# A hybrid decoder layer on one core: two pairs of output tiles by seven block products

## The chip, the cores and the metric

The kernel runs on one core of a Trainium2 chip. The metric is the device time of one execution in microseconds, taken over several runs as their median. The profile is of one execution of its own.

## The reference

One layer of a decoder, in float32, for 544 tokens (512 of a new sequence and 8 x 4 sample tokens) of 1024 channels:

```python
h = rmsnorm(x, g_pre_mix)
proj = jnp.einsum('btd,de->bte', h, w_in) + b_in        # conv, q, k, v, o, gates
y_conv = jnp.einsum('btc,cd->btd', silu(layernorm(depthwise_conv(glu(proj)))), w_conv_out)
y_m = jnp.einsum('btm,md->btd', mlstm_heads(proj), w_m_out)          # 2048 -> 1024
mix = jax.nn.sigmoid(gate_conv) * y_conv + jax.nn.sigmoid(gate_m) * y_m
x = x + rmsnorm(jnp.einsum('btd,de->bte', mix, w_o), g_post_mix)     # the output projection
hf = rmsnorm(x, g_pre_ff)
ff = jnp.einsum('btf,fd->btd', jnp.square(jax.nn.relu(hf @ w_ff1 + b_ff1)), w_ff2) + b_ff2
x = x + rmsnorm(ff, g_post_ff)
```

It also returns the new states of the convolution and of the mLSTM heads, which the change doesn't touch.

## The kernel before

**Layout.** Channels lie on the 128 partitions, tokens along the free dimension, so activations are 8 tiles (`KT`) of 128 x 544. A weight matrix is streamed as chunks of 128 output channels: `[128, 8, 128]`, 512 KB. A product of one chunk with 8 input tiles makes one output tile. For accuracy each operand is split into a high part rounded to fp32r and a low part, the rest; a product is three matmuls (high x high, high x low, low x high), and since the 544 tokens are cut in two halves of 272, a plain tile takes 8 x 3 x 2 = 48 matmuls of 272 columns.

**The ring of weights.** Every chunk has a number, its use. SyncE loads it into one of two raw buffers `wraw[0]`, `wraw[1]`; ScalarE rounds it into `whi[use % 4]` (function `hi`, L845), which is free when TensorE is through with use - 4 (`chunk_done`); VectorE subtracts to get `wlo` (`lo`, L1450) and with that frees the raw buffer (`lo_done`). TensorE waits for `lo_done` (`ring`). Both helper engines run three uses ahead of TensorE. Each engine's instructions are one queue in the order of the program text, and a wait holds all that is behind it; the order is written out by hand.

**Stages** in order of time: gated linear units, four mLSTM heads, gates, convolution output, memory output (`w_m_out`, C_MEM), output projection (`w_o`, C_OUT), MLP (C_FF).

**Seven products.** In the memory stage and in the MLP's second half some pairs of output tiles are made from 7 block products instead of 8: with the weights of two tiles and half of the inputs as a 2 x 2 block matrix, and the tokens' two halves as columns, Strassen's scheme in Winograd's form. `mem_seventh` (TensorE) makes P1, P7, P6, P5, P2, P4, P3 in this order from weight blocks X1 (P1, P7), X2 (P6, P5), X3 (P2, P4), X4 (P3), each product 4 x 3 matmuls of 272 columns. It needs sums of weight blocks (`mem_sum`, L1913 to L1922) and four sums of token blocks, which three VectorE steps make, then rounded by ScalarE and subtracted by VectorE. The banks of P1 and P7 are copied away by ScalarE before P2 and P4 add to them, and VectorE makes the part common to three results (`mem_common`) before P3. The memory pairs change between the banks `psum` (even) and `side` (odd).

**The output projection before.** `alternate` makes tiles 0 to 5 plain, each 48 matmuls, in `psum[0]` and `psum[1]` by turns. ScalarE squares (L853) and copies (L1183) each tile, VectorE adds up the squares (L2044). Tiles 6 and 7 are made by token halves: first the front half of both, then the back halves, so that the root of the front half's sum of squares (a matmul with ones, at step 3 of 8 of tile 6's back half; L1199, L1201) is ready early. Then VectorE, for each half, normalizes (L2061), adds the input (L2066) and makes low parts (L2072), which the MLP's first tiles wait for. The input comes back in one 2.1 MB load into `sgm` once all 8 mixed tiles are done. The mixed tiles `yc` (operands `bhi`, `blo`) are made in the memory stage: VectorE mixes a tile (`mix_even` L1989 to L1995, `mix_odd` L2001 to L2006), ScalarE rounds it (L1147), VectorE subtracts (L2011).

**The MLP's start.** 10 plain tiles; VectorE scales each pair's tiles by the root into `cq` (L2117, `plain_scaled`), ScalarE applies ReLU and square, and both make the 7 forms of it (`forms_made` L2125 to L2135; ScalarE L1279 to L1285). Then 27 units follow, the first with its weight splits `first_low` L2161, `sums_low` L2166, `second_low` L2173.

**The tail.** The last unit's results are squared, summed by matmuls with ones, the root is taken (L1410, L1412), then VectorE scales (L2289) quarter by quarter, the input is added (GpSimd L835 for the front half, VectorE L2301 for the back half), and each quarter is stored.

```python
def mem_bank(p, n):
    pairs = (psum[0], psum[1]) if p % 2 == 0 else (side[:, 0:2, :], side[:, 2:4, :])
...
for j in range(KT - 2):
    alternate(0, j, C_OUT, S_OUT, bhi, blo, (opnd_lo, 2 * KT) if j == 0 else None)
```

Of the kernel before, what the change touches and what calls it, by code (L numbers as in the profile page):

```python
# [12 lines left out]
P = 128  # L13
D_MODEL = 1024
KT = D_MODEL // P
SEQ = 512
# [30 lines left out]
C_FF = C_OUT + KT  # L47
# [43 lines left out]
_reads, _used, _splits = {"act": 2 * MEM_PAIRS, "dve": 2 * MEM_PAIRS}, {}, 0  # L91
# [14 lines left out]
def up_chunk(j):  # L106
    return C_FF - LATE + 2 * HID * (j // HID) + j % HID


def down_chunk(g, j):  # L110
    return C_FF - LATE + 2 * HID * (g // 2) + HID + 2 * j + g % 2


def mem_use(p, x):
    return C_MEM + len(MEM_USES) * p + MEM_USES.index(x)
# [96 lines left out]
def hybrid_layer(nc, xT, wstream, w_gates, cols, b_gates, b_v, w_dw, hist, c_in, n_in, m_in,  # L212
# [8 lines left out]
    with ctx:  # L221
# [158 lines left out]
        mem_s4 = at("mem_s4", [P, KT // 2, P], f32, late)  # L380
        mem_e = at("mem_e", [P, HALF], f32, late + TT * 4)
# [129 lines left out]
        def mem_raw_due(p, n):  # L511
            return 16 * (C_MEM // 2 + 2 * p + n + 1)

        def mem_bank(p, n):

            pairs = (psum[0], psum[1]) if p % 2 == 0 else (side[:, 0:2, :], side[:, 2:4, :])
            return pairs[n // 2][:, n % 2, 0:HALF]

# [4 lines left out]
        def mem_form(f, kt):  # L523

            if f < 3:
# [60 lines left out]
        def _(sp):  # L586
# [16 lines left out]
            def load(first, last, ahead=0):  # L603

                with sp.Fori(first, last) as i:
                    for s in range(2):
                        sp.wait_ge(lo_done, 2 * i + (s - 1 + ahead))
# [18 lines left out]
            load((C_OUT - LATE) // 2, (C_OUT - LATE + 4) // 2, LATE)  # L626

            sp.wait_ge(mixed, KT)
            sp.dma_start(sgm[:, :, :], xT).then_inc(x2_in, 16)
            load((C_OUT - LATE + 4) // 2, (C_FF - LATE) // 2, LATE)  # L630
# [11 lines left out]
            def unit_load(t):  # L642
# [7 lines left out]
                else:  # L650
                    sp.wait_ge(split_lo, SPLIT_AT[t - 2, "first"])
                    if is_down(t - 2):
                        sp.wait_ge(sum_made, MEM_SUMS * MEM_PAIRS + SUMS * order_of(t - 2) + SUMS - 1)
# [11 lines left out]
                if t >= 2:  # L665
                    sp.wait_ge(split_lo, SPLIT_AT[t - 2, "second"])
                    if is_down(t - 2):
                        sp.wait_ge(sum_made, MEM_SUMS * MEM_PAIRS + SUMS * order_of(t - 2) + SUMS)
# [15 lines left out]
            for g in range(2):  # L684
                part = slice(HALF * g, HALF * (g + 1))
                for half in range(2):
                    tiles = slice(KT // 2 * half, KT // 2 * (half + 1))
                    sp.wait_ge(out_pool if g == 0 else out_added, half + 1)
# [10 lines left out]
        def _(pool):  # L699
# [132 lines left out]
            for half in range(2):  # L832
                tiles = slice(KT // 2 * half, KT // 2 * (half + 1))
                pool.wait_ge(y_scaled, half + 1)
                pool.tensor_tensor(yacc[:, tiles, 0:HALF], yacc[:, tiles, 0:HALF], x1b[:, tiles, 0:HALF], ALU.add).then_inc(out_pool, 1)  # L835


        @block.scalar
        def _(act):
            def hi(i, per, k):  # L840

                act.wait_ge(raw_in[k % 2], 8 * per * i + 16 * ((k if k < C_OUT else k - LATE) // 2 + 1))
# [272 lines left out]
            def mem_rounded(p, x):  # L1115
# [12 lines left out]
                elif x == "X4":  # L1128
                    act.wait_ge(sum_made, MEM_SUMS * p + 4)
                    act.activation(whi[:, slot_, 0:KT // 2, :], mem_s4[:, :, :], ACT.Copy).then_inc(hi_done, 1)  # L1130
# [5 lines left out]
            def next_rounded(use):  # L1136

                if use < C_MEM or use >= C_OUT:
# [1699 lines left out]
```

## Time and profile before

| | us |
|---|---|
| median of 3 runs (1216.23 to 1217.03) | 1216.5 |
| the profiled execution | 1217.08 |
| its span, first to last instruction | 1215.6 |

| engine | busy us | share of the span |
|---|---|---|
| TensorE, matmuls | 1193.1 | 98% |
| TensorE, weight loads | 1121.5 | 92% |
| VectorE | 880.7 | 72% |
| ScalarE | 558.2 | 46% |
| GpSimd | 98.2 | 8% |

The page's chain of what ended last goes through TensorE for 93%, VectorE 3%, ScalarE 2%. The mean granted clock is 0.997 of full speed. The output projection lies between 780.4 and 829.2 us of the span.

How to read it: busy time says how full an engine is, not whether it holds the end. A wait in the profile is put down to the instruction that released it. The time of one instruction is from its start to its last write; two that don't depend on each other overlap by a little less than 0.1 us.

### The profile page before, as it was taken

The page shows a single profiled execution, that of the slowest core. Times are in us where ns is not written, and L with a number is a line of the kernel's source. Part 1 is how long each engine was busy: PE and PEld are TensorE (multiplying, and loading weights), DVE is VectorE, ACT ScalarE, POOL GpSimd, SP SyncE. Part 2 cuts the span into 40 slices and gives each one's busy share as a digit, 9 for nine tenths or more (in the row PEclk, how much of TensorE's full clock was granted, in tenths as well). Part 3 has the DMA queues.
Part 4 walks back from the last instruction along what each step waited for, and adds up shares of the span by engine and source line. Part 5 has one row for each costly group of instructions (what it writes and reads, how often), then busy time and mean ns, then how long its engine had stood idle before and what let it go on. Part 6 is the DMA issues. An engine that isn't in the chain of part 4 may idle for free.

```text
span 1215.6 us, 22805 instructions
## 1 busy us (share of the span) xinstructions
PE 1193.1 (98%) x8845; PEld 1121.5 (92%) x8845; DVE 880.7 (72%) x1329; ACT 558.2 (46%) x864; POOL 98.2 (8%) x163
## 2 busy tenths in 40 slices
PE   9999999999999999999999999999999999999995
PEld 9999978988797888879999999999999999999995
DVE  6933788988888888888458567538676577575796
ACT  7533443443355335335545333346655444354543
POOL 4120001101200110110000000000010010001111
PEclk9999999999999999999999999999999999999998
DMA  6344216516441751542322223431645445444662
GB/s 223 105 146 163 70 55 241 201 35 202 159 167 37 250 186 55 179 164 80 98 87 88 68 88 105 146 120 44 212 127 142 114 133 138 121 117 129 161 190 73
DMA packets 52623, 158.62 MB, mean 130 GB/s; under 512 B 5525, under 2 KB 7957, under 8 KB 52169
## 3 DMA queue, kind: packets, MB, share of 16 engines
q1 hardware_dynamic: 36376, 107.93, 27.2%
q0 software_dynamic: 16032, 49.62, 14.1%
q8 instruction: 50, 0.82, 0.3%
q14 instruction: 21, 0.16, 0.0%
q10 hardware_dynamic: 144, 0.09, 0.0%
HBM read 133.12 MB, written 24.49 MB: 130 GB/s over the span
## 4 chain that ended last, share of the span: by engine, by line
PE 93%; DVE 3%; ACT 2%; issue 1%; DMA 1%; DVEq 0%; ACTq 0%; SPq 0%
PE product L2307 68%; PE side L2307 24%; DMA wraw<-in_wstream 1%; ACT whi L845 0%; PE side L2492 0%; ACT yacc L1422 0%; DVE accp L1663 0%; ACT hhi L1285 0%; ACT cq L1265 0%; DVE wlo L1450 0%; DVE yacc L2192 0%; DVE hlo L2135 0%; DVE wlo L2167 0%; DVE cq L2117 0%; DVE wlo L2166 0%
## 5 line engine op out<-in xcount | busy, mean ns | idle before, releaser
L2307 PE MATMUL product<-ahi,whi 128*128 128x272 f32 x1232 | 261.7, 292 | 2.8 <-DVE cq L2117 1.6
L2307 PE MATMUL product<-ahi,wlo 128*128 128x272 f32 x1232 | 256.9, 288 | 0.0
L2307 PE MATMUL product<-alo,whi 128*128 128x272 f32 x1232 | 256.9, 288 | 0.0
L2307 PEld LDWEIGHTS product<-ahi,whi 128*128 128x128 f32 x1232 | 194.8, 188 | 13.2 <-issue 12.3
L1450 DVE TENSOR_TENSOR wlo<-wraw,whi 128x1024 fp32r<-128x1024 f32 x106 | 129.1, 1223 | 94.9 <-ACT whi L845 83.1
L2307 PEld LDWEIGHTS product<-alo,whi 128*128 128x128 f32 x1232 | 194.7, 189 | 0.0
L2307 PEld LDWEIGHTS product<-ahi,wlo 128*128 128x128 f32 x1232 | 193.5, 189 | 0.0
L845 ACT ACTIVATE whi<-wraw 128x1024 fp32r<-128x1024 f32 x106 | 111.1, 1054 | 159.5 <-PE product L2307 76.4
L1663 DVE SCALAR_TENSOR_TENSOR accp<-u,wdw,accp 128x512 f32<-128x512 f32 x240 | 163.6, 743 | 0.7 <-DVE accp L1663 0.7
L2307 PE MATMUL side<-hhi,whi 128*128 128x272 f32 x252 | 72.9, 289 | 1.8 <-DVE wlo L2161 1.3
L2307 PE MATMUL side<-hlo,whi 128*128 128x272 f32 x252 | 72.4, 287 | 0.0
L2307 PE MATMUL side<-hhi,wlo 128*128 128x272 f32 x252 | 72.4, 287 | 0.0
L828 POOL DMA_DIRECT2D wraw<-in_wstream x16 | 13.8, 863 | 595.9 <-DMA wraw<-in_wstream 595.9
L1309 ACT ACTIVATE whi<-wraw 128x1024 fp32r<-128x1024 f32 x27 | 28.6, 1059 | 69.7 <-PE side L2307 34.9
L2307 PE MATMUL product<-hhi,whi 128*128 128x272 f32 x196 | 56.6, 289 | 0.6 <-DVE hlo L2135 0.4
L2307 PE MATMUL product<-whi,ahi 128*128 128x512 f32 (+1 forms) x160 | 56.6, 354 | 0.0
L2307 PE MATMUL product<-hlo,whi 128*128 128x272 f32 x196 | 56.4, 288 | 0.0
L2307 PE MATMUL product<-hhi,wlo 128*128 128x272 f32 x196 | 56.3, 287 | 0.0
L2307 PE MATMUL product<-wlo,ahi 128*128 128x512 f32 (+1 forms) x160 | 55.8, 349 | 0.0
L2307 PE MATMUL product<-whi,alo 128*128 128x512 f32 (+1 forms) x160 | 55.8, 348 | 0.0
L2307 PE MATMUL product<-blo,whi 128*128 128x272 f32 x256 | 55.5, 288 | 0.0
L2307 PE MATMUL product<-bhi,whi 128*128 128x272 f32 x256 | 55.5, 288 | 0.0
(418 smaller groups left out, 2630.4 us busy)
## 6 DMA issues: line engine op xcount, KB each, us to landing
wraw<-in_wstream SPq DMA_DIRECT2D x176, 512.0 KB, 3.7
crg<-in_c_in POOLq DMA_DIRECT2D x32, 512.0 KB, 6.8
out_c_s<-crg POOLq DMA_DIRECT2D x32, 512.0 KB, 3.2
wraw<-in_wstream POOLq DMA_DIRECT2D x16, 256.0 KB, 4.1
s<-in_wstream SPq DMA_DIRECT2D x15, 256.0 KB, 3.9
s<-in_wstream POOLq DMA_DIRECT2D x15, 256.0 KB, 6.2
hb<-head_rows POOLq DMA_DIRECT2D x4, 580.0 KB, 5.3
x<-in_xT SPq DMA_DIRECT2D x4, 544.0 KB, 6.5
```

The lines of the kernel that those rows point to most:

```text
L828: pool.dma_start(raw_of(t)[:, 0, KT // 2:KT, :], wstream[one, :, 0:KT // 2, :], accum_op=ALU.add).then_inc(s3_in[d % 2], 16)
L845: act.activation(whi[:, k % RING, :, :], wraw[:, k % 2, :, :], ACT.Copy).then_inc(hi_done, 1)
L1309: act.activation(whi[:, 2, :, :], raw_of(t)[:, 1, :, :], ACT.Copy).then_inc(split_hi, 1)
L1450: V.tensor_tensor(wlo[:, k % RING, :, :], wraw[:, k % 2, :, :], whi[:, k % RING, :, :].bitcast(f32), ALU.subtract).then_inc(lo_done, 1)
L1663: ins = V.scalar_tensor_tensor(sum_, src, w, sum_, ALU.mult, ALU.add)
L2307: return pe.matmul(out, lhsT, rhs, start=start, stop=stop, skip_group_check=check)
```

## The change

In the output projection, tiles 0 and 1 stay plain and come first, in the `side` banks. Tiles 2 to 5 are made as two pairs (numbers 4 and 5 behind the memory pairs 0 to 3) of seven products each by `mem_seventh`. Tiles 6 and 7 are as before. The uses become T0, T1, X1 to X4 of pair 4, X1 to X4 of pair 5, 6, 7: twelve instead of eight, from the same bytes. Four sets of token sums are made from the mixed tiles kt and kt + 4 (`token_sums`, three VectorE steps into `fr[:, 2:4]`; `token_sums_rounded`, ScalarE; `token_sums_rest`, VectorE), the first of them within the memory stage's last pair. Their buffers are the ones of memory operands no longer read. Results are put together by `out_common` and `out_made` into `y`, and squared and scaled from there by `out_scaled`. The last mixed tile is made by `last_mixed`, with the multiplication by the gate done on the two parts before the last product is there. The memory pairs swap their banks: 0 and 2 in `side`, 1 and 3 in `psum`.

Five changes of order: the sum `asmp` one gated tile earlier; `plain_scaled(2, 0)` ahead of the last low part of the first forms; `first_low(0)` and `first_split(0)` ahead of the last step of forms 3; in the tail, three of ScalarE's six gains behind the first squares and the first root, with `scaled_half(0, 0)` waiting only for four gains; and GpSimd adds the input to two tiles of the back half.

```diff
@@ banks
-            pairs = (psum[0], psum[1]) if p % 2 == 0 else (side[:, 0:2, :], side[:, 2:4, :])
+            pairs = (psum[0], psum[1]) if p in (1, 3, 4) else (side[:, 0:2, :], side[:, 2:4, :])
@@ SyncE
+            def out_load(q, s):
+                one = late + 2 + 2 * q
+                halves = wstream[one:one + 2, :, :, :].rearrange("a p (h k) m -> h p a (k m)", h=2)
+                if q == 0:
+                    sp.wait_ge(lo_done, C_OUT + s + 1)
+                else:
+                    sp.wait_ge(lo_done, mem_use(MEM_PAIRS, ("X2", "X3")[s]) + 1)
+                    if s == 1:
+                        sp.wait_ge(sum_made, MEM_SUMS * (MEM_PAIRS + 1))
...
+            for s in range(2):
+                out_load(0, s)
             sp.wait_ge(mixed, KT)
             sp.dma_start(sgm[:, :, :], xT).then_inc(x2_in, 16)
+            for s in range(2):
+                out_load(1, s)
@@ ScalarE
+                    if x == "Y1" and p == MEM_PAIRS - 1:
+                        token_sums_rounded(0)
...
+            def out_scaled(j):
+                act.wait_ge(drained[j % 2], S_OUT + j // 2 + 1)
+                squares(j + 2 * KT, tile(y, j), j % 2)
+                act.wait_ge(sq_ready, 2 * KT + j + 1)
+                act.activation(tile(y, j), tile(y, j), ACT.Copy, scale=c("g_post_mix", j))
+            def out_kept(p):
+                act.wait_ge(chunk_done, mem_use(p, "X1") + 1)
+                if p > MEM_PAIRS:
+                    act.wait_ge(drained[1], S_OUT + 2)
...
+            token_sums_rounded(1)
+            next_rounded(C_OUT + 3)
+            for kt in range(2, KT // 2):
+                token_sums_rounded(kt)
+            next_rounded(C_OUT + 4)
+            out_copied(0)
+            for p in range(MEM_PAIRS, ALL_PAIRS):
+                next_rounded(mem_use(p, "X1") + 3)
+                if p == MEM_PAIRS:
+                    out_copied(1)
+                out_kept(p)
+                next_rounded(mem_use(p, "X2") + 3)
+                if p > MEM_PAIRS:
+                    out_scaled(2)
+                    out_scaled(3)
+                next_rounded(mem_use(p, "X3") + 3)
+                next_rounded(mem_use(p, "X4") + 3)
+            out_scaled(4)
+            out_scaled(5)
+            next_rounded(C_FF + 1)
@@ ScalarE, tail
-            for j in range(KT - 2):
...
+            for j in range(KT // 2 - 1):
+                early_gain(j)
             act.wait_ge(y_summed, 2)
             half_square(0, 0, 0)
             half_square(1, 1, 0)
+            early_gain(KT // 2 - 1)
+            half_root(0)
+            for j in range(KT // 2, KT - 2):
+                early_gain(j)
@@ VectorE
+                if last:
+                    token_sums(0)
+                    mem_sum(p + 1, 0)
+                    token_sums_rest(0)
                 mix_even(p, ready_at)
...
+            def token_sums(kt):
...
+                dve.wait_ge(mixed, kt + KT // 2 + 1)
...
+                    dve.wait_ge(mem_lo, 3 * KT // 2 + kt)
...
+            token_sums(1)
+            mem_sum(p, 1)
+            token_sums_rest(1)
+            token_sums(2)
             dve.wait_ge(sq_added, 2 * KT)
             n = mark(V.memset(sqs[:, :], 0.0))
             dve.wait_ge(dve_step, n)
+            token_sums_rest(2)
+            token_sums(3)
+            token_sums_rest(3)
+            next_rest(C_OUT + 3)
+            next_rest(C_OUT + 4)
+            out_squared(0)
+            for p in range(MEM_PAIRS, ALL_PAIRS):
+                last = p == ALL_PAIRS - 1
+                if last:
+                    out_made(p - 1)
+                mem_sum(p, 2)
+                next_rest(mem_use(p, "X1") + 3)
+                if not last:
+                    out_squared(1)
+                    mem_sum(p + 1, 0)
+                if last:
+                    out_common(p)
+                next_rest(mem_use(p, "X2") + 3)
+                if not last:
+                    out_common(p)
+                    mem_sum(p + 1, 1)
+                next_rest(mem_use(p, "X3") + 3)
+                if last:
+                    out_squared(2)
+                    out_squared(3)
+                if not last:
+                    next_rest(mem_use(p, "X4") + 3)
+            out_made(ALL_PAIRS - 1)
+            next_rest(C_FF)
+            out_squared(4)
+            out_squared(5)
+            lo(0, 4, C_FF + 1)
@@ TensorE
-            for j in range(KT - 2):
-                alternate(0, j, C_OUT, S_OUT, bhi, blo, (opnd_lo, 2 * KT) if j == 0 else None)
+            for j in range(2):
+                w = ring(0, 4, C_OUT + j)
+                free(j, S_MEM + MEM_PAIRS - 1)
...
+            for p in range(MEM_PAIRS, ALL_PAIRS):
+                for name in MAIN:
+                    ins = mem_seventh(p, name)
```

## Rows read from the trace of the kernel before

**Rows 1.** What TensorE waited for, whole span: us in total, times, longest us.
```profile
PE product L2307 <- DVE cq L2117: 1.6, 1, 1.6
...
PE side L2307 <- DVE wlo L2161: 1.3, 1, 1.3
PE product L2307 <- DVE asmp L1626: 1.2, 1, 1.2
PE product L2307 <- DVE yc L1970: 1.0, 1, 1.0
```

**Rows 2.** Stretch of six tiles: us, PE, PEld, DVE, ACT, POOL, clock, DMA, GB/s.
```profile
780.41:816.53 36.12, 36.12 (x290) 36.12 (x289) 14.36 (x17) 12.50 (x17) 0.00 (x0) 1.00 0.46 161
```

**Rows 3.** Chain that ended last, MLP units: start us, us, what.
```profile
929.95 10.50 PE product L2307 x84
940.45 12.00 PE side L2307 x96
```

**Rows 4.** Timeline, token sums of the MLP: start us, us, engine, line, operation.
```profile
864.21 0.72 DVE L2125 TENSOR_TENSOR tt<-cq 128x544 f32<-128x544 f32 x1
864.96 0.44 DVE L2127 TENSOR_TENSOR tt<-cq,tt 128x272 f32<-128x272 f32 x1
...
868.31 1.29 DVE L2135 TENSOR_TENSOR hlo<-tt,hhi 128x1088 fp32r<-128x1088 f32 x1 [1.23 <-ACT hhi L1285]
...
867.18 1.10 ACT L1285 ACTIVATE hhi<-tt 128x1088 fp32r<-128x1088 f32 x1
```

**Rows 5.** Timeline of VectorE, memory pair 3, low parts of X2.
```profile
750.65 0.69 DVE L1897 TENSOR_TENSOR wlo<-mem_s,whi 128x512 fp32r<-128x512 f32 x1 [1.28 <-ACT whi L1127]
751.26 0.68 DVE L1898 TENSOR_TENSOR wlo<-wraw,whi 128x512 fp32r<-128x512 f32 x1
```

**Rows 6.** Timeline of VectorE, turn from memory to output projection.
```profile
771.14 1.23 DVE L1450 TENSOR_TENSOR wlo<-wraw,whi 128x1024 fp32r<-128x1024 f32 x1 [1.39 <-ACT whi L845]
774.43 0.44 DVE L1989 TENSOR_TENSOR fr<-side,mem_e 128x272 f32<-128x272 f32 x1 [2.06 <-PE side L2307]
...
780.44 0.44 DVE L2001 TENSOR_TENSOR fr<-side,mem_e 128x272 f32<-128x272 f32 x1 [2.28 <-PE side L2307]
...
783.48 0.72 DVE L2011 TENSOR_TENSOR blo<-yc,bhi 128x544 fp32r<-128x544 f32 x1 [0.73 <-ACT bhi L1147]
```

**Rows 7.** Timeline, end of the output projection, ScalarE, then VectorE.
```profile
816.60 0.62 ACT L853 ACTIVATE fr<-product 128x544 f32<-128x544 f32 x1 [3.85 <-PE product L2307]
817.12 0.71 ACT L1183 ACTIVATE y<-product,col 128x544 f32<-128x544 f32 x1
...
823.04 0.44 DVE L2057 TENSOR_TENSOR sqs<-sqs,fr 128x272 f32<-128x272 f32 x1 [2.56 <-ACT fr L1189]
825.39 0.44 DVE L2061 TENSOR_TENSOR y<-y,rst 128x272 f32<-128x272 f32 x1 [1.90 <-ACT rst L1201]
```

**Rows 8.** DMA issues of this stage: count, KB each, us to landing.
```profile
wraw<-in_wstream SPq DMA_DIRECT2D x23, 512.0 KB, 3.6
sgm<-in_xT SPq DMA_DIRECT2D x1, 2176.0 KB, 9.0
```

**Rows 9.** Timeline around MLP unit 0, VectorE, then TensorE.
```profile
869.52 0.72 DVE L2117 TENSOR_TENSOR cq<-product,rst 128x544 f32<-128x544 f32 x1
...
898.38 0.69 DVE L2166 TENSOR_TENSOR wlo<-s,whi 128x512 fp32r<-128x512 f32 x1 [1.23 <-ACT whi L1302]
...
895.94 0.39 PE L2307 MATMUL side<-hhi,whi 128*128 128x272 f32 x1 [1.27 <-DVE wlo L2161]
```

**Rows 10.** Timeline of ScalarE at a table load, start of the heads.
```profile
112.54 1.28 ACT L960 ACT_TABLE_LOAD   x1
113.83 0.72 ACT L960 ACTIVATE mcol<-side 32x4 f32<-32x4 f32 x4
```

**Rows 11.** Timeline of the tail, ScalarE, GpSimd, VectorE.
```profile
1195.74 3.94 ACT L1422 ACTIVATE yacc<-yacc,col 128x544 f32<-128x544 f32 x6
...
1204.00 4.94 POOL L835 TENSOR_TENSOR yacc<-yacc,x1b 128x1088 f32<-128x1088 f32 x2 [33.15 <-DVE yacc L2289]
...
1208.86 2.48 DVE L2301 TENSOR_TENSOR yacc<-yacc,x1b 128x1088 f32<-128x1088 f32 x2
```

More of the change, by code:

```diff
@@ L46 @@
 LATE = C_OUT - (C_MEM + 2 * KT)
-C_FF = C_OUT + KT
+OUT_PAIRS = 2
+OUT_USES = ("X1", "X2", "X3", "X4")
+C_PAIRS = C_OUT + 2
+C_FF = C_PAIRS + len(OUT_USES) * OUT_PAIRS + 2
+AHEAD = C_FF - C_OUT - KT
+ALL_PAIRS = MEM_PAIRS + OUT_PAIRS
 HID = 16
@@ L601, in _, with load @@
             sp.dma_start(nold[:, :, :, :], n_in).then_inc(const_in, 16)
-            def load(first, last, ahead=0):
+            def load(first, last):
                 with sp.Fori(first, last) as i:
                     for s in range(2):
-                        sp.wait_ge(lo_done, 2 * i + (s - 1 + ahead))
+                        sp.wait_ge(lo_done, 2 * i + (s - 1))
                         sp.dma_start(wraw[:, s, :, :],
@@ L687, in _ @@
                     tiles = slice(KT // 2 * half, KT // 2 * (half + 1))
-                    sp.wait_ge(out_pool if g == 0 else out_added, half + 1)
+                    if g == 0 or half == 0:
+                        sp.wait_ge(out_pool, 3 if g else half + 1)
+                    if g == 1:
+                        sp.wait_ge(out_added, half + 1)
                     sp.dma_start(yT[:, tiles, part], yacc[:, tiles, part]).then_inc(out_saved, 16)
@@ L2133, in forms_made @@
                 V.tensor_tensor(hlo[i][:, 1:3, :], q[:, 2:4, :], hhi[i][:, 1:3, :].bitcast(f32), ALU.subtract).then_inc(form_lo, 1)
+                if before_last is not None:
+                    before_last()
                 dve.wait_ge(form_hi, 3 * p + 3)
@@ L2287, in scaled_half @@
                 dve.wait_ge(tail_root, 2 * g + 2)
-                dve.wait_ge(y_gained, KT - 2 + 2 * g + 2)
+                dve.wait_ge(y_gained, KT // 2 if g == 0 and half == 0 else KT - 2 + 2 * g + 2)
                 V.tensor_tensor(yacc[:, tiles, part], yacc[:, tiles, part],
@@ L2298, in _ @@
             for half in range(2):
-                tiles = slice(KT // 2 * half, KT // 2 * (half + 1))
+                tiles = slice(KT // 2 * half + 2 * (1 - half), KT // 2 * (half + 1))
                 dve.wait_ge(y_scaled, half + 3)
@@ L2614, in mem_seventh @@
                     for s in range(2):
-                        free(s, S_MEM + max(p - 1, 0))
+                        if p > 0:
+                            free(s, S_MEM + p - 1 if p < MEM_PAIRS else S_OUT + p - MEM_PAIRS)
                 elif not opens:
@@ L2650, in _ @@
                     mem_plain(p, m).then_inc(chunk_done, 1)
-            for j in range(KT - 2):
-                alternate(0, j, C_OUT, S_OUT, bhi, blo, (opnd_lo, 2 * KT) if j == 0 else None)
+            for j in range(2):
+                w = ring(0, 4, C_OUT + j)
+                free(j, S_MEM + MEM_PAIRS - 1)
+                for kt in range(KT):
+                    if j == 0:
+                        pe.wait_ge(opnd_lo, 2 * KT + kt + 1)
+                    for n, (a, b) in enumerate(((whi, bhi), (whi, blo), (wlo, bhi))):
+                        for g in range(2):
+                            ins = mm(piece(in_side(j), g), a[:, w, kt, :], b[:, kt, slice(*PARTS[g])],
+                                     kt == 0 and n == 0, kt == KT - 1 and n == 2)
+                ins.then_inc(chunk_done, 1)
+            for p in range(MEM_PAIRS, ALL_PAIRS):
+                for name in MAIN:
+                    ins = mem_seventh(p, name)
+                    if name in ("P7", "P5", "P4", "P3"):
+                        ins.then_inc(chunk_done, 1)
             def half_part(s, w, g, xhi, xlo, kt):
```

186 lines of the change are left out of this document (136 added, 50 removed).

## The prediction

> **What bounds the kernel.** The page's first part gives the matmul engine 98% of the span, and its chain of what ended last lies 93% on it, so only what shortens or delays TensorE's queue moves the end. The view of what TensorE waited for shows how little is left there: four of its longer waits, 1.2, 1.0, 1.6 and 1.3 us [rows 1], are those that four of the edits aim at. Next comes the table by stretch for the output projection: its first six tiles take 36.1 us without a gap [rows 2], and its two half-by-half tiles follow at 816.5. Last, the timelines of VectorE and ScalarE there, because the new scheme puts work on them that TensorE had so far not waited for. The granted clock is 1.00 there [rows 2], that is the 2.4 GHz level, and the change gives TensorE no idle stretch long enough that I expect it to fall.
>
> **The fewer products.** A unit of two plain tiles takes 12.00 us for 96 matmuls, a unit of seven block products 10.50 for 84 [rows 3], 0.125 us a matmul. The output projection's two new pairs leave out 2 x 12 matmuls: -3.0 us. Their weight bytes stay the same (eight chunks), only cut otherwise.
>
> **The work that comes with them.** For each of four row pairs VectorE makes token sums in three dependent steps, 0.72, 0.44 and 0.44 us, ScalarE rounds them (1.10), VectorE takes the rest (1.29), all in the forms of [rows 4]. A step that waits for another starts some 0.04 us after its end, one that doesn't 0.08 before it (864.21 + 0.72 against 864.96 [rows 4], and 750.65 + 0.69 against 751.26 [rows 5]). One set is thus 0.72 + 0.44 + 0.44 + 1.10 + 1.29 plus four hand-overs: 4.1 us. The sums lie in one buffer, so the sets can't overlap. I follow them on the clock of the trace of before.
>
> *Turn from memory to output.* VectorE ends the rest of the second output chunk at 772.4 and began to mix tile 6 at 774.4 [rows 6]. Set 0 and the pair's first weight sum (0.69) now stand between: 1.6 for the sums, to 773.9, rounding until 775.1, rest until 776.4. The mix starts at 776.3, 1.9 later. VectorE had 2.3 us of idle time ahead of the last tile [rows 6] that take this in, and the last mix is cut by one wait, so the low part of tile 7 ends at 784.5 where it ended at 784.2 [rows 6]. TensorE wants it 42 matmuls after 780.4, at 785.7: nothing lost.
>
> *Sets 1 to 3* then run in a row: 784.4 + 4.2 + 4.1 + 4.1, ending at 797.0. The two weight sums of X2 (0.69 each) and the clearing of the squares lie inside the waits for ScalarE. Tiles 0 and 1 end at 780.4 + 12.1 = 792.5, P1 at 794.0, and P7 wants set 3 at 795.1. It waits 1.9 us. Queued behind the set is the rest of X2, two halves of 0.69 [rows 5], ready at 798.2 while P7 is through at 797.5: 0.7 us more. Behind that VectorE has the rest of X3 (1.23), a sum of squares (0.72) and the fourth sum (0.69), until 800.5. On ScalarE the rounding of X4 waits for that sum, and behind it stand the square and the copy of tile 1 (0.62 and 0.71 [rows 7]) and only then the copy of P1's bank, which ends at 802.7. P2 asks for it at 801.3: 1.4 us. P3 asks for the common part at 805.8; VectorE, held by the X1 block of the second pair, whose load leaves at 798.2 and takes 3.6 us [rows 8], has it at 806.4: 0.6 us. The second pair costs 0.3 us once more at its P2, where the copy waits for the first pair's results and the fourth sum. Together 4.9 us, and 0.1 us for each restart (an estimate: the first matmul behind a wait lasts 0.39 us [rows 9], the others 0.29): 5.4. The half tiles start at 816.5 - 3.0 + 5.4 = 818.9, 2.4 us later than before. The 2.1 MB load of the input, 9.0 us [rows 8], is issued once the last tile is mixed, and runs when no weight load is wanted: nothing.
>
> *End of the stage.* Before, ScalarE squared and copied tile 5 as soon as it was there, at 816.6 [rows 7], and was through before the first half was. Now VectorE makes tiles 4 and 5 in four steps, but stands until 821.5 behind the low part of the last chunk, which was asked for only after the fourth sum (813.4 + 3.6, then 1.0 until ScalarE is through with tiles 2 and 3, 1.06 and 1.23), and behind two sums of squares. ScalarE then has squares and copies of two tiles (2.6 us), a weight rounding (1.06), the first half's square and copy and the table load (1.28) before it can square the second half at 827.9; VectorE adds it by 828.8. TensorE asks for that sum at 826.1: 2.7 us. Before it asked at 823.7 (816.5 and 57 matmuls) and had it from 823.5 (823.04 + 0.44 [rows 7]), so it didn't wait. The root is ready 5.2 us later than before, VectorE's row of normalizing steps, which sets the next stage, starts at 825.39 + 5.2 [rows 7], and all behind it moves with it. So the stage costs +5.2 (-3.0 and +8.2), which I take. Its bounds: each of some sixty VectorE steps 0.03 us shorter or longer in the same order of steps gives +3.4 and +7.0.
>
> The table load lets the next instruction start 0.01 us after its end [rows 10]. The Trainium skill, page "ScalarE: Activation LUTs", section "What ACT_TABLE_LOAD costs", sets a drain of about 1.38 us behind the load. With that the stage would cost +6.6 and the kernel end at 1219.6; this trace doesn't agree, and no run here shows such a drain.
>
> **The edits of order.** (1) The sum of the sample's columns moves ahead of the last gated tile: VectorE idles ahead of that tile, and TensorE, with nothing else left to wait for, keeps the 1.2 us [rows 1]: -1.2, and the heads behind run on TensorE's own pace. If a transfer paced them it would be 0. (2) The memory pairs swap their banks, so pair 0 opens banks that nobody holds: the wait of 1.0 for yc L1970 goes, -1.0. (3) The third plain tile is scaled before the last rest of the forms, at 867.1 (its forms' second rest ends there) instead of 869.5 [rows 9], and TensorE's 1.6 goes. (4) The first split of unit 0 moves ahead of the last forms, and the 1.3 goes. But (3) and (4) pay nothing: from the MLP's first forms on VectorE and ScalarE hand work to each other, and the only idle time in each row is that of waiting for the other, as at 868.31 [rows 4] and 898.38 [rows 9]. (3) takes one step of 0.64 out of that row. (4) makes VectorE wait 0.6 for ScalarE and puts both sums_low and the scaling of tile 4 behind the moved forms. The low part of the sums, two halves of 0.69 from 898.38 on [rows 9], ended at 899.7, and does again, and TensorE, early by 2.8, waits for it. 0, with -0.5 and +0.5 as ends. (5) The tail: of six gains in a row (3.94 us [rows 11]) ScalarE does three, then the squares. Of the 1.9 us that the other three take, 0.5 goes to a wait for VectorE; the first root comes 1.3 earlier, but the postponed gains leave only 0.7 at the second half's scaling. One quarter of the last additions goes to GpSimd, whose four tiles take 2.47 us, while VectorE's take 1.24 [rows 11], so VectorE's last ends another 0.6 earlier: -1.3. GpSimd's added piece runs beside VectorE's; before, the two met for only 0.1 us (1208.86 against 1204.00 + 4.94 [rows 11]). If VectorE had to wait it out, the tail would give -0.6. The Trainium skill, page "SBUF — State Buffer", section "Who interferes with whom", says that a VectorE instruction with two inputs in SBUF contends with GpSimd's reads. By that the -0.6 would hold; no row here tests it.
>
> **Sum.** +5.2 - 1.2 - 1.0 + 0 - 1.3 = +1.7 us. The profiled execution took 1217.08 us with a span of 1215.6, 0.6 above the median of 1216.5; the difference goes onto the median: 1218.2.
>
> **Rivals.** *A, faster: the two helper engines keep up.* If the sets, copies and last squares were ready when TensorE asks, the stage would give its 3.0 and the sum be -6.5: 1210.0. For it speaks that VectorE is busy for only 14.4 of the 36.1 us and ScalarE for 12.5 [rows 2]. Against it, that the sets are one dependent chain, and that VectorE gets 12.5 us of added work in a 12 us stretch. If half the waits at the pairs stay, 1212 to 1214. *B, slower: VectorE's row at the turn is longer than its rows.* TensorE pays one for one for whatever delays set 3. Each 0.1 us on a set costs 0.3, and with +7.0 for the stage and edit (1) worth nothing beyond 1.0, the result is 1220.2. It decides from 0.7 us more than my 5.2; for it speaks that many of these steps wait for two engines. *C, edits (3) and (4) pay after all:* if TensorE and not the row of the two engines set the start of unit 0's sums, -2.8: 1215.4. Against it speak the two idle times just named, each ended by the other engine. *D:* that seven products aren't fewer in time is excluded by the 10.50 against 12.00.
>
> **Chances.** Forecast 0.50 (own range 1216 to 1219.7), A 0.19, B 0.25, C 0.06. A measurement here tells about 0.2%, 2.4 us. Faster by that (below 1214.1): A, 0.18, and little of the rest, 0.20. Slower (above 1218.9): B and a quarter of the forecast, 0.38. Within: 0.42. The range 1212 to 1221.5 leaves out most of A and the end of B.
>
> **What would show it.** Right: a wait of some 2 us for a rest of token sums inside the first pair's P7, one of over 1 us for the copy of its P1 bank, 2 to 3 us for the sum of squares between the last half tiles, and the waits for asmp, yc and cq gone while one for the sums of unit 0 takes the place of the latter. Wrong: the half tiles starting before 816.5 on this clock, or the heads' start giving nothing.

## The result and the profile after

The changed kernel takes 1222.2 us (median of 5 runs, 1221.6 to 1223.2), the kernel before, run beside it, 1217.0 (1216.2 to 1219.3): the ratio is 1.0042, with a 95% interval of 1.0030 to 1.0053. That is 0.4% slower, 4.0 us above the forecast of 1218.2 and 0.7 above the end of its range. The profiled execution took 1223.0 us with a span of 1221.5, 5.9 longer than the span before.

What TensorE waited for in the changed kernel (us in total, times, longest):

```profile
PE side L2525 <- DVE wlo L2381: 3.1, 1, 3.1
PE side L2525 <- DVE sqs L2269: 2.9, 1, 2.9
PE product L2525 <- DVE out_tlo L2163: 2.3, 1, 2.3
...
PE product L2525 <- DVE y L2210: 0.6, 1, 0.6
PE product L2525 <- DVE wlo L2005: 0.6, 1, 0.6
```

The waits for asmp, yc and cq at the first forms [rows 1] are gone. In their place stand three longer ones, each where the forecast had put it: the rest of token sums in the first pair (1.9 forecast, 2.3 measured), the sum of squares between the last half tiles (2.7 and 2.9), and the sums of unit 0 (early by 2.8, so 2.8 and 3.1). They add up to about what was forecast. What was not forecast stands in the table by stretch, here for the few microseconds around and behind each wait (us, TensorE's busy time and matmuls, granted clock, share and GB/s of the DMA engines):

```profile
792.60:796.40 3.80, 0.96 (x7) 1.00 0.00 0
796.40:801.00 4.60, 4.60 (x24) 0.63 0.58 175
...
828.30:832.00 3.70, 3.70 (x20) 0.55 0.12 48
...
906.20:910.20 4.00, 4.00 (x22) 0.57 0.10 18
```

Behind each of the three waits the granted clock falls towards 0.50, the 1.2 GHz level, for some 3.4 us. TensorE is busy all through it, with 20 to 24 matmuls where 0.125 us each would let it do 30 to 37. In the kernel before the clock was 1.00 up to the last matmul. The chain of what ended last shows the price at the last two places, first in the kernel before, then in the changed one (start, us, what):

```profile
824.27 4.89 PE product L2307 x39
...
899.73 7.74 PE side L2307 x60
```

```profile
828.34 6.44 PE product L2525 x39
...
905.35 9.28 PE side L2525 x60
```

The same 39 matmuls take 1.55 us more, the same 60 take 1.54 more.

**Where the 5.9 us came from**, by the starts of the same pieces in the two traces. Heads' start 112.71 to 111.58: -1.1. End of the memory stage 780.41 to 778.20: another -1.1. VectorE's first normalizing step 825.39 [rows 7] to 829.46: +6.3 on top of the -2.2, against +5.2 forecast. The slow stretch behind it: +1.5. Unit 0's 60 matmuls: +1.6, nearly all of it the second slow stretch. Tail: -1.3. Together -2.2 + 6.3 + 1.5 + 1.6 - 1.3 = 5.9. The forecast's sum was 1.7; the missing 4.2 are the two slow stretches (3.1) and the stage's 1.1. The 5.9 is the difference of two single executions; the medians differ by 5.2. Each of the two traces has one stray delay of 0.7 us in the heads, at different places; in this account they cancel.

The end of the output projection in the changed kernel (timeline, ScalarE and VectorE; in brackets the idle time before and what ended it):

```profile
816.50 1.04 ACT L899 ACTIVATE whi<-wraw 128x1024 fp32r<-128x1024 f32 x1
...
817.57 1.23 DVE L1556 TENSOR_TENSOR wlo<-wraw,whi 128x1024 fp32r<-128x1024 f32 x1 [2.38 <-ACT whi L899]
818.72 1.55 DVE L2197 TENSOR_TENSOR sqs<-sqs,fr 128x544 f32<-128x544 f32 x2
820.18 0.43 DVE L2218 TENSOR_SCALAR y<-side 128x272 f32<-128x272 f32 x1
...
821.00 0.66 ACT L907 ACTIVATE fr<-y 128x544 f32<-128x544 f32 x1 [1.21 <-DVE y L2219]
...
825.39 1.28 ACT L1317 ACT_TABLE_LOAD   x1
826.68 0.40 ACT L1289 ACTIVATE fr<-product 128x272 f32<-128x272 f32 x1
...
827.12 0.44 DVE L2269 TENSOR_TENSOR sqs<-sqs,fr 128x272 f32<-128x272 f32 x1 [0.79 <-ACT fr L1289]
```

The order of things is the forecast's: VectorE stands for the last chunk's rounding, then adds two squares, and only then makes tiles 4 and 5 (from 820.2; forecast 821.5, less the 2.2 gained by then: 819.3). Square, copy, rounding and table load follow on ScalarE, and the second half's sum comes at 827.6. And again ScalarE's next instruction starts 0.01 us after the table load.

### The profile page after: what moved, and what is told of

It is laid out like the page before. It is cut to its first block, busy times and chain, and to the rows that moved or that the text cites. A ratio compares the mean times of both kernels' runs of the same rounds, so it can differ in the third digit from the quotient of the medians.

```text
span 1221.5 us, 22817 instructions
## 1 busy us (share of the span) xinstructions
PE 1196.3 (98%) x8821; PEld 1124.5 (92%) x8821; DVE 905.9 (74%) x1375; ACT 567.2 (46%) x880; POOL 99.5 (8%) x164
## 4 chain that ended last, share of the span: by engine, by line
PE 86%; DVE 6%; ACT 4%; issue 3%; DMA 1%; DVEq 0%; ACTq 0%; SPq 0%
PE product L2525 61%; PE side L2525 24%; DMA wraw<-in_wstream 1%; ACT whi L899 1%; ACT hhi L1385 1%; DVE wlo L1556 0%; ACT cq L1365 0%; DVE out_tlo L2163 0%; DVE hlo L2349 0%; PE side L2710 0%; DVE accp L1770 0%; ACT out_thi L1224 0%; DVE fr L2153 0%; DVE cq L2329 0%; DVE sqs L2197 0%
## 5 line engine op out<-in xcount | busy, mean ns | idle before, releaser
L1556 DVE TENSOR_TENSOR wlo<-wraw,whi 128x1024 fp32r<-128x1024 f32 x102 | 124.3, 1223 | 87.7 <-ACT whi L899 76.0
L899 ACT ACTIVATE whi<-wraw 128x1024 fp32r<-128x1024 f32 x102 | 106.8, 1053 | 151.1 <-PE product L2525 75.9
L1409 ACT ACTIVATE whi<-wraw 128x1024 fp32r<-128x1024 f32 x27 | 28.6, 1060 | 69.5 <-PE product L2525 34.8
L1892 DVE SCALAR_TENSOR_TENSOR crg<-crg,hb,product 128x1024 f32<-128x1024 f32 x32 | 40.6, 1278 | 16.0 <-PE product L2525 16.0
L2525 PEld LDWEIGHTS side<-hhi,whi 128*128 128x128 f32 x252 | 48.2, 191 | 4.3 <-DVE wlo L2381 3.4
```

Of the source, the lines that this page charges most:

```text
L899: act.activation(whi[:, k % RING, :, :], wraw[:, k % 2, :, :], ACT.Copy).then_inc(hi_done, 1)
L1409: act.activation(whi[:, 2, :, :], raw_of(t)[:, 1, :, :], ACT.Copy).then_inc(split_hi, 1)
L1556: V.tensor_tensor(wlo[:, k % RING, :, :], wraw[:, k % 2, :, :], whi[:, k % RING, :, :].bitcast(f32), ALU.subtract).then_inc(lo_done, 1)
L1892: V.scalar_tensor_tensor(crg[:, n % C_RING, :, :], crg[:, n % C_RING, :, :], hb[:, R_DEC + b:R_DEC + b + 1], psum[s][:, :, :], ALU.mult, A ...
L2525: return pe.matmul(out, lhsT, rhs, start=start, stop=stop, skip_group_check=check)
```

## The experiments

Each run has its ratio to the kernel before, measured beside it: 1216.7 us for the runs up to filled and for the four after it, 1216.8 for tuned and the two with made stands, 1217.7 for tail_alone. In brackets stand the ratio and its 95% interval. The changed kernel was measured only beside the 1217.0 of the result; so a difference of medians to it can be 0.3 us too large. The names are those under which the expectations speak of them.

**Edits of order without the pairs.** order_three has the edits of asmp, banks and tail; order_all has those at the MLP's start too. Both have a plain output projection:

```diff
 order_three, against before
+            for j in range(2):
...
+            for j in range(2, KT - 2):
+                alternate(0, j, C_OUT, S_OUT, bhi, blo)
 order_all, against order_three
-            forms_cross(3)
             first_split(0)
+            forms_cross(3)
...
-            forms_made(0)
-            cq_free(0)
-            plain_scaled(2, 0)
+            forms_made(0, third_scaled)
...
-            forms_made(3)
             first_low(0)
+            forms_made(3)
```

> The kernel before with three of the edits of order (the sum asmp, the swap of the memory banks, the tail) and with the output projection plain: tiles 0 and 1 in side, 2 to 5 in product. Both theories expect what the three gave in the trace of after: -1.1 for the heads' start, -0.6 to -1.0 for the banks, -1.3 for the tail, so 1217.0 - 3.2 = 1213.8, and a granted clock of 1.00 at the MLP's start. If one of them gave its gain in after only because something behind it moved, the time is above 1215.

> The same with the two edits at the MLP's start as well (third tile's scaling and first split earlier): all the edits of order, no pairs. The forecast's reckoning (the two edits are worth 0, VectorE's and ScalarE's row sets the start of unit 0's sums): 1213.8, the same as order_three. The theory of the clock (one wait of about 2.9 us in the place of two of 1.6 and 1.3 lets the granted clock fall behind it): a wait of 2.8 to 3.1 us ahead of unit 0's P6, granted clock near 0.5 to 0.7 in the 3 us behind it, and +1.5 against order_three: 1215.3. The forecast's rival C (the two edits pay 2.8): 1211.0.

Measured: order_three 1212.75 us (0.9968, 0.9956 to 0.9980), order_all 1214.46 (0.9984, 0.9975 to 0.9993). Here is what TensorE waited for at the MLP's start, order_all, then order_three:

```profile
PE side L2330 <- DVE wlo L2186: 3.1, 1, 3.1
```

```profile
PE side L2324 <- DVE wlo L2178: 1.3, 1, 1.3
PE side L2324 <- DVE wlo L2184: 0.5, 1, 0.5
```

And the stretch behind the waits, order_all, then order_three:

```profile
896.40:900.40 4.00, 3.77 (x19) 0.61 0.37 65
```

```profile
896.80:900.80 4.00, 4.00 (x33) 1.00 0.87 209
```

The two edits gather order_three's waits (1.6 for cq, then 1.3 and 0.5) into one of 3.1 and a short one of 0.4, and the clock falls behind the long one. They cost 1.7 us: the slowest of order_three's six times is 1213.5, the fastest of order_all's eleven 1214.0. Rival C, by which they would pay 2.8, is out. The three other edits are worth 4.0 us together, 0.5 more than the forecast's 3.5.

**The same two edits undone in the changed kernel**, no_34:

> The kernel after with the same two edits undone: pairs and the other edits stay. Clock theory: the waits of 1.6 and 1.3 are back, the clock stays at 1.00 there, and the time is 1.5 below after: 1220.7. The forecast's reckoning: the same as after, 1222.2. Rival C: 2.8 above after, 1225.

Measured: 1220.85 us (1.0033, 1.0021 to 1.0046), 1.35 below the changed kernel by the medians, 1.1 by the ratios. The intervals overlap, so this time alone proves little. But the waits of 1.6 and 1.3 are back and the clock stays at 1.00 there, as in order_three. So the loss by these two edits doesn't depend on the pairs. From order_three to no_34 only the pairs are added: +8.1 us where the forecast had +5.2.

**TensorE kept busy in its waits.** filled puts small matmuls ahead of the waits:

```diff
+                    if p == MEM_PAIRS and name == "P7" and kt == KT // 2 - 1:
+                        for _ in range(24):
+                            mm(mem_bank(p, BANK["P6"])[:, 0:P], ones[:, :], ones[:, :], True, True)
```

> The kernel after with small matmuls of ones by ones (128 x 128 x 128) ahead of its three long waits, into banks that are opened anew behind them: 24 inside P7 of pair 4, 30 ahead of the sum of squares between the last half tiles, 32 ahead of unit 0's P6. They are meant to end before the wait does, so that nothing is later for them. Clock theory (the granted clock falls because TensorE stands): clock 1.00 in all three stretches, half tiles starting at most 0.3 earlier (the wait for the copy of P1's bank, 1.2 to 1.5 us, appears in place of the slow stretch), the root 1.5 to 1.8 earlier, unit 0's matmuls behind their wait another 1.5 earlier: 1222.2 - 3.2 = 1219.0. If the clock falls for another reason (what the helper engines or the DMA queues do at that moment), it falls here too and the time is 1222.2 or up to 0.5 above.

Measured: 1231.2 us (1.0125, 1.0109 to 1.0140). A failed experiment for its purpose. Each filler took 0.23 us, in two passes, so 24 lasted 5.5 us in a wait of 2.3. And the 30 meant for the sum of squares stood one sum too late, where nothing had to be waited for. It left one thing to learn: the wait for the first sum was still there, and this time the clock stayed up behind it.

```profile
826.34 0.73 PE L2525 MATMUL side<-sqs,ones 128*128 128x272 f32 x2 [2.88 <-DVE sqs L2269]
```

```profile
826.30:830.30 4.00, 3.96 (x29) 1.00 0.25 101
```

filled_short has 9, 11 and 12 fillers, the second lot at the right sum:

> The kernel after with ones by ones matmuls (each took 0.23 us in filled) in TensorE's three long waits, this time short enough to end inside them: 9 in P7 of pair 4 (wait 2.3), 11 ahead of the front half's sum of squares (2.9), 12 ahead of unit 0's P6 (3.1). Clock theory, in which a stand lowers the granted clock: 1.00 in all three stretches and -3.1 to -3.4 against after, 1219.0 (the first one gives little, since a wait of some 1.3 for the copy of P1's bank comes in its place). Rival (what falls with the stand is something the helper engines or the queues do at that time): low clock as in after, 1222.2 to 1222.5. A second rival, from filled, where a stand of 2.9 ahead of the same sum had a clock of 1.00 behind it: a stand lowers the clock only at some moments, and filling one changes the others; then at least one low stretch of some 3.4 us stays.

Measured: 1219.18 us (1.0021, 1.0012 to 1.0030), below the changed kernel by 3.0 us by the medians and 2.6 by the ratios; the intervals just touch. The traces say 3.0: from VectorE's first normalizing step to the end it is 392.0 us in the changed kernel (829.46 to 1221.5) and 389.0 here (828.82 to 1217.8). The same three stretches, now with the clock at 1.00:

```profile
796.40:801.00 4.60, 3.29 (x26) 1.00 0.71 221
...
828.00:832.00 4.00, 4.00 (x34) 1.00 0.03 11
...
903.00:907.00 4.00, 3.76 (x30) 1.00 0.39 62
```

and the longest wait of the whole middle is one that the forecast had and the changed kernel had not:

```profile
PE product L2525 <- ACT mem_e L1262: 1.3, 1, 1.3
```

Nothing was done but to give TensorE useless work while it waited (and to let it wait for the fillers' banks first), and nothing it needs comes earlier. So the low clock follows from the standing, and it costs some 3 us. The first stretch costs nearly nothing, because TensorE, once fast, must wait 1.3 us for the copy of P1's bank: that is the forecast's "P2 asks for it at 801.3: 1.4 us". ScalarE's and VectorE's steps from there to the root are all 0.65 us earlier than in the changed kernel, but they were so already before the first filler, by the stray delay in the heads of that trace.

**The two places of the pairs mended.** All on top of no_34. ends: another order at the end of the stage. sets: each set of token sums with a buffer of its own.

```diff
 ends, ScalarE
                 if p > MEM_PAIRS:
-                    out_scaled(2)
-                    out_scaled(3)
+                    out_squares(2)
+                    out_squares(3)
                 next_rounded(mem_use(p, "X3") + 3)
+                if p > MEM_PAIRS:
+                    out_scaled(2)
+                    out_scaled(3)
+                    out_squares(4)
+                    out_squares(5)
                 next_rounded(mem_use(p, "X4") + 3)
...
             o_root(0, o_stat, 1)
+            out_scaled(4).then_inc(y_front, 1)
+            out_scaled(5).then_inc(y_front, 1)
 sets
+        def tok_at(kt):
+
+            return corners(fr[:, 2:4, :] if kt == 0 else y[:, 2 * kt:2 * kt + 2, :])
...
-                tt4 = corners(fr[:, 2:4, :])
+                tt4 = tok_at(kt)
```

> The kernel no_34 with the end of the output projection put in another order: ScalarE squares tiles 2 and 3 and rounds the last chunk before it scales them, squares tiles 4 and 5 at once and scales them behind the root; VectorE adds their squares and makes tiles 4 and 5 before the last chunks' low parts; the table load comes after the front half's last square. My reckoning from the rows of after: ScalarE reaches the second half's square at 822.8 instead of 826.7, TensorE asks for its sum at 823.2 or 824.7 and waits at most 0.5, so the 2.9 goes and with it the low clock behind it (1.5): 1220.9 - 3.9 = 1217.0. If the low clock there has nothing to do with the stand: -2.4 only, 1218.5. If some other chain of helper steps is as late: no gain, 1220.9.

> The kernel no_34 with the sums of token blocks 1 to 3 in buffers of their own (the places of y that are not written before tile 2 is there), so that a set need not wait for the rest of the one before; VectorE makes sums 1, 2, then rest 1, sums 3, rests 2 and 3. The forecast's reckoning (one buffer makes the four sets one chain): set 3 ends some 3 us earlier, at about 792.2, the waits of 2.5 and 0.6 in P7 are gone and so is the low clock behind them; the wait for the copy of P1's bank comes up with 0 to 1.4. Half tiles start 2.5 to 4.5 earlier; of it all reaches the end if the end of the stage follows: 1217.4 (-3.5, 1216.4 to 1218.4). Rival (VectorE's sum of work sets the pace, not the chain): set 3 at 794 or later, -1 at most, 1219.9.

> ends and sets together. Theory: the gains add, since they lie at different waits: 1220.9 - 3.9 - 3.5 = 1213.5 (1211.5 to 1215), about as order_three with its plain tiles (1212.8), and the pairs' 3.0 us are then eaten by what waits are left. If one engine's total work is the bound, one of the gains is lost: 1217.

Measured: ends 1216.76 us (1.0002, 0.9992 to 1.0011), 4.1 below no_34. sets 1218.00 (1.0010, 1.0001 to 1.0019), 2.9 below it. both 1214.42 (0.9980, 0.9971 to 0.9989), 6.4 below it. In ends the wait for the sum of squares is down from 2.9 to 0.2, in sets the one for the sums of tokens is gone. These are the longest waits left in the stage, ends, then sets:

```profile
PE product L2531 <- DVE out_tlo L2171: 2.2, 1, 2.2
```

```profile
PE side L2523 <- DVE sqs L2271: 2.9, 1, 2.9
PE product L2523 <- ACT mem_e L1266: 1.3, 1, 1.3
```

The last rest of the token sums in sets shows that the single buffer, and not VectorE's sum of work, had made set 3 late; it ends at 792.0, in no_34, on which sets is built, at 794.4 (in the changed kernel at 795.1, with the stray delay of its heads):

```profile
790.67 1.29 DVE L2165 TENSOR_TENSOR out_tlo<-y,out_thi 128x1088 fp32r<-128x1088 f32 x1
```

The gains nearly add: 4.1 + 2.9 = 7.0 against 6.4. ends alone still has one low stretch in the stage (behind 2.2 + 0.6), sets one (behind 2.9), both has none there.

**The order inside the pairs**, tuned, on top of both:

```diff
             out_copied(0)
+            out_copied(1)
             for p in range(MEM_PAIRS, ALL_PAIRS):
-                next_rounded(mem_use(p, "X1") + 3)
-                if p == MEM_PAIRS:
-                    out_copied(1)
                 out_kept(p)
+                next_rounded(mem_use(p, "X1") + 3)
```

> The kernel both with the order inside the two pairs changed too: ScalarE copies tile 1 and then the banks of P1 and P7 before it rounds X4; VectorE makes the common part before the low part of X4, clears the squares after X2 and X3, and makes tiles 2 and 3 before X2 of the second pair. Theory (every wait in the pairs is an order of helper steps, and what is left behind them is the second pair's weights, landing at 796.1 and 798.5): the waits of 0.6, 1.3, 0.6 and 0.3 of both become about 0.6 and 0.6 at the second pair's first weights, 1214.4 - 1.7 = 1212.7, which is order_three's 1212.8: the pairs then pay for themselves and no more. If the loads don't hold it back: 1211.5. If VectorE's steps only change places: 1214.4.

Measured: 1212.46 us (0.9966, 0.9952 to 0.9979). The waits left in the stage:

```profile
PE side L2532 <- DVE wlo L2016: 0.6, 1, 0.6
PE side L2532 <- DVE wlo L2013: 0.4, 1, 0.4
PE side L2532 <- DVE sqs L2307: 0.2, 1, 0.2
PE product L2532 <- DVE wlo L2016: 0.2, 1, 0.2
```

tuned is as fast as order_three (1212.75), and their intervals are nearly the same: with most of the waits gone, the pairs give back what they cost and no more that can be measured. Of their 3.0 us, 1.4 go to these four waits, two of them at the second pair's first weights, and 0.3 is the difference of the medians; where the rest goes wasn't followed.

**How long a stand lowers the clock.** stands and stands_two are order_three with GpSimd holding TensorE back at 12 and 11 tiles:

```diff
+            for n, chunk in enumerate(STANDS):
+                pool.wait_ge(chunk_done, chunk)
+                for m in range(STAND_OPS[n]):
...
+                    pool.memset(causal[:, :], 0.0).then_inc(stood if m == STAND_OPS[n] - 1 else stand_step, 1)
```

> The kernel order_three, with GpSimd holding TensorE back ahead of twelve of the 24 tiles of the gates and the convolution output, two tiles apart: chains of 4, 6, 8, 10, 12, 14, 14, 12, 10, 8, 6 and 4 small memsets, some 1.0 to 3.7 us each. Nothing is left out. Theory of the clock, as the waits of the real kernels bear it out (2.0 and less had a clock of 1.00 behind them, 2.3 + 0.6 to 3.1 mostly a low one, once, in filled, not): stands up to 2.0 have none, those above 3 all have a stretch of some 3.4 us at the lower level behind them that costs 1.5 to 1.7, those between only some, by where they fall. If the length alone decided, the two stands of one length would always be alike.

> The same with eleven stands of 9 and 11 memsets by turns (some 2.3 and 2.9 us), in other places. If the length decides, all of one length are alike; if the place in time does too, only some of them have the low clock behind them, more of the longer.

Measured: 1256.8 and 1258.8 us, one execution each. By the length of TensorE's wait, in order of length:

| stands of | number | with a low clock behind |
|---|---|---|
| 0.8 to 1.7 us | 5 | 0 |
| 2.2 to 2.5 us | 7 | 6 |
| 2.7 to 3.0 us | 7 | 5 |
| 3.3 and 3.8 us | 4 | 4 |

One stand of 2.73 and one of 2.21, both in stands, and the stretches behind them:

```profile
681.30:685.30 4.00, 4.00 (x32) 1.00 0.41 127
...
695.70:700.70 5.00, 4.98 (x27) 0.66 0.36 109
```

The longer one cost nothing, the shorter one lost a third of the clock over 5 us, 1.7 us. Length alone doesn't decide, as filled had hinted. In stands_two five stands had the same length, 2.99, and four of them had the low clock behind. Two stands (2.99 and 3.79) had twice the usual length of low clock, 6.8 us. There it began 0.7 and 0.8 us before TensorE started again; in order_all and behind the other stand of 3.79 it began 0.5 before and had the usual length.

The expectation's "2.0 and less had a clock of 1.00 behind them" is not what all the traces show. The edit of the tail makes one of TensorE's waits there longer, from 1.3 to 2.0, ahead of the last sum of squares. In the changed kernel the four matmuls behind it run at full clock, in both the clock falls 0.07 us after they begin:

```profile
1210.60 1.19 PE L2525 MATMUL product<-cq,ones 128*128 128x272 f32 x4 [1.97 <-ACT cq L1502]
```

```profile
1201.79 2.15 PE L2533 MATMUL product<-cq,ones 128*128 128x272 f32 x4 [1.97 <-ACT cq L1514]
```

The chain of both goes through these four, so this execution ended 1.0 us later for it. In no_34 the clock fell 0.8 us behind the wait and the four took 1.44. In the other eleven traces with this wait of 2.0 they took the usual 1.2.

**The tail**, tail_alone: order_three without GpSimd's share of the last additions.

```diff
-            pool.wait_ge(y_scaled, 3)
-            pool.tensor_tensor(yacc[:, 0:2, HALF:TT], ..., ALU.add).then_inc(out_pool, 1)
```

> The kernel order_three without GpSimd's share of the last additions: VectorE adds the input to all eight tiles of the back half, as before; the other parts of the tail's edit stay. In order_three VectorE's addition of half the size (544 elements) took 1.22 us beside GpSimd's of 1.32, and the one of full size 1.28. If the two hold each other up on the way to the same memory, the share gives next to nothing: the two additions here take 1.28 each, VectorE ends within 0.1 of where it did, and the time is 1212.8 (1212.6 to 1213.2). The forecast's reckoning (VectorE's last 0.6 earlier by the share): 1213.4.

Measured: 1213.35 us beside a kernel before of 1217.66, a ratio of 0.9966 (0.9954 to 0.9978), order_three's 0.9968 over again. The share is worth nothing. In the changed kernel the groups by shape show why:

```profile
L2519 DVE TENSOR_TENSOR yacc<-yacc,x1b 128x1088 f32<-128x1088 f32 x1 | 1.3, 1277 | 0.0
L2519 DVE TENSOR_TENSOR yacc<-yacc,x1b 128x544 f32<-128x544 f32 x1 | 1.2, 1222 | 0.0
...
L2411 DVE TENSOR_TENSOR yacc<-yacc,common 128x544 f32<-128x544 f32 x2 | 1.4, 722 | 0.0
```

```profile
1214.49 1.32 POOL L889 TENSOR_TENSOR yacc<-yacc,x1b 128x544 f32<-128x544 f32 x1
```

VectorE's addition of 544 elements, started at 1215.18, took 1.22 us where the same form takes 0.72 elsewhere. GpSimd's own was under way until 1215.81. VectorE lost 0.5 us to it, the very time the share should have saved. That it was GpSimd's access to the same memory that held VectorE up is an inference from this overlap; no run moved the one against the other.

## Why the prediction was wrong, point by point

- **The clock: the step that failed.** "... and the change gives TensorE no idle stretch long enough that I expect it to fall." The forecast put the clock at nothing. The change gave TensorE three such stretches, which the same text had priced at 1.9 to 2.8 us each, and the clock fell behind all three. Two of the slow stretches lay on the path, 1.55 and 1.54 us by the chain; filled_short takes some 3 us back. No row of the trace before spoke for that sentence. Its waits on full work were 1.6 at most [rows 1], so that a stand of 2 to 3 us wasn't tested there and should have been bounded from both sides, as the other unseen costs were. With the price that only these runs show, 1.5 us for each of two stands, the forecast would have been 1218.2 + 3.1 = 1221.3; the 0.9 that is left is about the stage's 1.1 (below).
- **Fewer products, -3.0:** nothing speaks against it. tuned, with 1.4 us of waits left in the stage, ends 0.3 below the plain order_three.
- **Sets of token sums:** right in kind and size. The wait was 2.3 (1.9 forecast) and 0.6 behind it for X2 (0.7), and sets showed that the shared buffer was its cause. The recorded row has a slip: 784.4 + 4.2 + 4.1 + 4.1 is 796.8, not 797.0. On the other side a set took 4.3 us (the rests end at 790.8 and 795.1) and not 4.1; set 3 came 0.3 later than forecast.
- **Copy of P1's bank, 1.4:** not seen in the changed kernel, since TensorE was slow just then, and seen at 1.3 as soon as it was fast (filled_short). Common part 0.6, second pair 0.3: as forecast.
- **End of the stage, 2.7:** measured 2.9, but all of it later. The root came +6.3 behind and not +5.2: the half tiles started 0.7 later than reckoned (817.4, against 818.9 less 2.2), and ScalarE began its last tiles 0.9 later. This is within the stage's bounds (+3.4 to +7.0); it is the size that was off, and this is the second term that missed: +5.2 forecast, +6.3 measured. Why each step of the row was a little longer wasn't followed; it isn't the slow stretch inside the pairs, since filled_short has the same row without it.
- **Edits (1) and (2):** -1.1 and -1.1 against -1.2 and -1.0.
- **Edits (3) and (4), 0:** the mechanism was right, TensorE came early and waited 3.1 for the sums of unit 0, and rival C fell. What was missing is that the wait, in one piece, costs more than in two: +1.7 in order_all, outside the -0.5 and +0.5.
- **Tail, -1.3:** the sum came out right (-1.3) by luck, with wrong parts. The earlier root gave 0.9 (1206.46 to 1212.77, less 7.2 of delay by then), not 0.7. The additions gave nearly nothing, not 0.6, and some 0.4 came between VectorE's last addition and the end (4.2 us before, 3.9 now). tail_alone has this too (3.8), so it doesn't come from GpSimd's share; what brings it wasn't tried by itself. Nor had the forecast seen that the edit lengthens the wait ahead of the last sum to 2.0, which cost 1.0 us in the trace of both. The forecast had weighed the case that VectorE must wait GpSimd out and had not believed it; it is what happened. The Trainium skill, page "SBUF — State Buffer", section "Who interferes with whom", says so too: the two engines share one pair of ports, and a VectorE instruction with two inputs in that memory contends with a GpSimd instruction that reads it. This trace agrees, 1.22 against 0.72 us.
- **Rival B** (VectorE's row longer, 1220.2, deciding from 0.7 us more) is the nearest to what came: the stage's row was 1.1 longer. Its place fits in part: 0.3 of the 1.1 was there at set 3 and 0.7 when ScalarE rounded the last chunk (816.50, forecast 818.0 less 2.2). But it would have left the time 2 us short of what was measured.
- **Rival A** (the helpers keep up, 1210.0) fell for the kernel as it was. tuned comes near its case by another order of steps, at 1212.5.
- **The table load:** 0.01 us from its end to the next instruction, as in [rows 10]. The drain that the Trainium skill sets behind it (page "ScalarE: Activation LUTs", section "What ACT_TABLE_LOAD costs") isn't seen here either.

## What to carry to other kernels

A wait of TensorE has two prices, its length and the slow matmuls behind it; where a reckoning comes to a stand longer than any that the trace shows at full clock, bound the second price too. Where waits can't be removed, several short pieces can be cheaper than one long one: here the edit that merely gathered them lost 1.7 us. Before a scheme with fewer products is judged by the products, follow its helper steps' buffers and the order at the stage's end: here the same pairs cost 8.1 us as they were, 1.7 once each set of sums had its own place and squares went ahead of copies, and nothing measurable once the banks were copied earlier too.

## What the runs showed of the hardware

- The granted clock went to its lower level (1.2 GHz) behind 15 of 18 made stands of 2.2 to 3.8 us, and behind none of 5 of 0.8 to 1.7 us. Behind a wait of 2.0 in the tail it fell at once in one trace (both, four matmuls in 2.15 us instead of 1.19), after 0.8 us in another (no_34), and in the other eleven not in time to slow these matmuls. In the dense matmuls it usually stayed low for 3.4 us, worth 1.5 to 1.7 us.
- Between 2.0 and 3.0 us it isn't settled which stands are hit. What decides besides the length stays open; no run varied the moment of a stand alone.
- Matmuls of ones by ones, 0.23 us each, were enough to keep the clock at 1.00 through three waits of 2.3 to 3.1 us (filled_short).
- VectorE's addition of two operands in the on-chip memory took 1.22 us instead of 0.72 beside a GpSimd addition that it overlapped by 0.6.
